# Down-projection weights in runs of four neighbouring rows per partition, with strided PE transposes to match

## The reference

```
def swiglu(h, w_gate, w_up, w_down):
    return (jax.nn.silu(h @ w_gate) * (h @ w_up)) @ w_down
...
    for e in range(N_EXPERTS):
        y = y + gates[:, e:e + 1].astype(t.dtype) * swiglu(t, w_gate[e], w_up[e], w_down[e])
```

## Time and profile before

| | us |
|---|---|
| median of 3 runs | 1413.0 (1412.39 to 1413.77) |
| the profiled execution, its time | 1415.45 |
| the profiled execution, its span | 1413.7 |
| TensorE matmul busy | 1386.3 (98%) |
| VectorE busy | 1121.7 (79%) |
| ScalarE busy | 941.2 (67%) |
| HBM read | 428.33 MB |

### The profile page before, as it was taken

How to read it: one execution, slowest core, us unless ns; L and a number is a source line. 1 busy time by engine, 2 the same in 40 slices (tenths; PEclk the granted TensorE clock), 3 DMA queues, 4 the chain that set the end, 5 groups by cost and what they waited for, 6 DMA issues and landing times. The chain is left out here.

```text
span 1413.7 us, 16873 instructions
## 1 busy us (share of the span) xinstructions
PE 1386.3 (98%) x6454; PEld 1118.3 (79%) x6454; DVE 1121.7 (79%) x1298; ACT 941.2 (67%) x1248; POOL 123.7 (9%) x117
## 2 busy tenths in 40 slices
PE   7999999999999999999999999999999999999998
PEld 4886788886786788888888888888888888887886
DVE  2565545553655599999999899999999999999996
ACT  3544534443545387887787787787887788779773
POOL 2041000001031100000000040000001000000600
PEclk9999999999999999999999999999999999999999
DMA  9324555527114599999999999999999999999992
GB/s 355 121 97 157 200 188 188 198 78 295 49 72 178 192 393 394 390 395 397 391 393 395 388 393 395 395 393 394 393 397 395 394 392 393 394 395 397 396 390 103
DMA packets 180680, 435.25 MB, mean 308 GB/s; under 512 B 5556, under 2 KB 10356, under 8 KB 180468
## 3 DMA queue, kind: packets, MB, share of 16 engines
q1 hardware_dynamic: 177540, 423.11, 79.7%
q0 software_dynamic: 3056, 11.02, 2.0%
HBM read 428.33 MB, written 5.78 MB: 307 GB/s over the span
## 5 line engine op out<-in xcount | busy, mean ns | idle before, releaser
L2100 DVE TENSOR_TENSOR unit_rounded<-wmem,unit_rounded 128x1024 fp32r<-128x1024 f32 (+1 forms) x744 | 851.9, 1206 | 56.3 <-ACT unit_rounded L1484 55.3
L1484 ACT ACTIVATE unit_rounded<-wmem 128x1024 fp32r<-128x1024 f32 (+1 forms) x744 | 719.9, 1044 | 120.0 <-PE ps L1162 46.5
L1023 PE MATMUL ps<-unit_rounded,vbuf_rounded 128*128 128x512 f32 x472 | 184.1, 390 | 0.0
L1025 PE MATMUL ps<-unit_rounded,stage_rounded 128*128 128x512 f32 x472 | 183.9, 390 | 0.0
L1024 PE MATMUL ps<-unit_rounded,vbuf_rounded 128*128 128x512 f32 x472 | 183.8, 389 | 0.0
L1160 PE MATMUL ps<-unit_rounded,hT_rounded 128*128 128x512 f32 x448 | 177.7, 397 | 0.0
L1162 PE MATMUL ps<-unit_rounded,hT_rounded 128*128 128x512 f32 x448 | 174.9, 390 | 0.0
L1161 PE MATMUL ps<-unit_rounded,hT_rounded 128*128 128x512 f32 x448 | 174.6, 390 | 0.0
L1160 PE MATMUL ps<-unit_rounded,qkT_rounded 128*128 128x512 f32 x336 | 133.4, 397 | 0.8 <-DVE qkT_rounded L2289 0.8
L1162 PE MATMUL ps<-unit_rounded,qkT_rounded 128*128 128x512 f32 x336 | 131.1, 390 | 0.0
L1161 PE MATMUL ps<-unit_rounded,qkT_rounded 128*128 128x512 f32 x336 | 131.0, 390 | 0.0
(11 more groups left out here) (286 smaller groups left out, 1781.8 us busy)
## 6 DMA issues: line engine op xcount, KB each, us to landing
wmem<-in_w_exp_gate_dram SPq DMA_DIRECT2D x56, 2048.0 KB, 12.6
wmem<-in_w_exp_up_dram SPq DMA_DIRECT2D x56, 2048.0 KB, 13.2
wmem<-in_w_exp_down_dram SPq DMA_DIRECT2D x56, 2048.0 KB, 13.2
wmem<-in_w_in_dram SPq DMA_DIRECT2D x4, 3072.0 KB, 17.3
wmem<-in_w_ff_up_dram SPq DMA_DIRECT2D x5, 2048.0 KB, 8.9
wmem<-in_w_ff_gate_dram SPq DMA_DIRECT2D x5, 2048.0 KB, 7.6
wmem<-in_w_ff_down_dram SPq DMA_DIRECT2D x5, 2048.0 KB, 7.6
wmem<-in_w_out_dram SPq DMA_DIRECT2D x4, 2048.0 KB, 8.0
```

The costliest lines, as they stand in the source:

```text
L1023: pe.matmul(o, hhb, hi[:, b, c], start=(first and b == 0), stop=False, skip_group_check=True)
L1025: mm = pe.matmul(o, hlb, hi[:, b, c], start=False, stop=(b == blocks - 1), skip_group_check=True)
L1484: act.activation(quarter_r(HIGH[l][0 if last else kind], q, cols), quarter(SETS[l][i][kind], q, cols), ACT.Copy).then_inc(hi_ready[kind], 1)
L2100: dve.tensor_tensor(quarter_r(u, q, cols), quarter(u, q, cols), quarter_r(HIGH[l][0 if last else kind], q, cols), ALU.subtract).then_inc(l ...
```

## The change

The 512 rows of a down piece are dealt to the partitions in runs: partition p gets rows `4p` to `4p + 3`, which are neighbours in memory, so its 16 KB are one contiguous piece in HBM and in SBUF. In the dense step with 256 rows it is two rows and 8 KB. Slot k of the partitions then holds rows `4p + k`. So that the hidden columns on the partitions are the same rows, block b of the transposes reads the columns `b, b + 4, b + 8, ...` of `hid` (every second column in the small dense step) in place of 128 neighbours. Gate and up loads, the matmuls, the writes to PSUM and everything else stay.

```diff
+        def dealt(a, cols, b):
+
+            return a[:, 0:cols].rearrange("t (p k) -> t k p", p=P)[:, b, :]
...
             def load_down(w, l, i, f0, rows=FT):
-                sp.dma_start(unit(SETS[l][i][2], rows // P, D), w[f0:f0 + rows, :].rearrange("(k p) c -> p k c", p=P)) \
+                sp.dma_start(unit(SETS[l][i][2], rows // P, D), w[f0:f0 + rows, :].rearrange("(p k) c -> p k c", p=P)) \
                     .then_inc(s_raw[i][2], 16)
...
                 if kind < 2:
                     dst = unit(SETS[1][i][kind], KD, FT)
-                    src = (w_exp_gate, w_exp_up)[kind][0, ds(e, 1), :, f0:f0 + FT]
+                    src = (w_exp_gate, w_exp_up)[kind][0, ds(e, 1), :, f0:f0 + FT].rearrange("o (k p) c -> p (o k) c", p=P)
                 else:
                     dst = unit(SETS[1][i][2], FT // P, D)
-                    src = w_exp_down[0, ds(e, 1), f0:f0 + FT, :]
-                sp.dma_start(dst, src.rearrange("o (k p) c -> p (o k) c", p=P)).then_inc(s_raw[i][kind], 16)
+                    src = w_exp_down[0, ds(e, 1), f0:f0 + FT, :].rearrange("o (p k) c -> p (o k) c", p=P)
+                sp.dma_start(dst, src).then_inc(s_raw[i][kind], 16)
...
                 for b in range(cols // P):
-                    mm = pe.transpose(ps[:, 2 * bufs, b * P:(b + 1) * P], hid[bufs][:, b * P:(b + 1) * P], ident)
+                    mm = pe.transpose(ps[:, 2 * bufs, b * P:(b + 1) * P], dealt(hid[bufs], cols, b), ident)
                 mm.then_inc(t_full, count)
...
                 for b in range(FT // P):
-                    mm = pe.transpose(ps[:, 2 * (m % 2), b * FEW:(b + 1) * FEW], hid[m % 2][0:FEW, b * P:(b + 1) * P],
+                    mm = pe.transpose(ps[:, 2 * (m % 2), b * FEW:(b + 1) * FEW], dealt(hid[m % 2][0:FEW, :], FT, b),
                                       ident[0:FEW, 0:FEW])
                 mm.then_inc(t_full, 2)
```

## The result

The changed kernel takes **1418.24 us** (median of 6 runs, 1417.71 to 1419.16); the kernel before, beside it, 1413.11 us (6 runs, 1412.39 to 1413.77). The ratio is 1.0031, 95% interval 1.0021 to 1.0041: slower by 0.3%, 5.1 us by the medians. The prediction said 1414.8 and that no difference would be seen. The time lies in its range of 1411 to 1441, but that range reached so far up only for a rival, a load at a quarter of the rate, that did not come; above the forecast's own 1417.5 the prediction had no case that fits.

A forecast was written before the change was run, and what follows sets the result against it. The prediction took TensorE to bound the kernel, with the DMA just behind. Its terms, -0.6 us for loads and +2.4 for transposes, gave +1.8: 1417.25 us on the profiled execution, 1414.8 against the median; range 1411 to 1441.

The forecast's parts named there:

- a load at a quarter of the rate: Rival: strided transpose loads take 228 ns and outlast their stream, +26.9 us, 1439.9 us; chance 0.22.
- the forecast's own 1417.5: Upper end of the forecast's own range from 1411.5 us, set by a strided load of 120 ns.
- What bounds the kernel: Expert stage: TensorE sets the time, DMA just behind; DMA gains mostly hidden, TensorE losses not; gathers costed at 0.
- The loads: 56 expert down loads at 427 GB/s, giving back 13.5 us of DMA time, nearly all hidden; -0.6 us paid out.
- The term for the last step: Last step: down piece lands 0.24 us earlier, shortening TensorE's wait before the last transposes; -0.6 us.
- The rival of slower long pieces: Down loads take 0.5 us longer each and the DMA sets the pace; +20, 1433 us; chance 0.05.
- the one without any effect on the DMA: Rival: down pieces are cut to 4 KB on their way, only transposes count; +2.4, 1415.4 us; chance 0.05.
- The rival of a larger gain: Whole last-step gap and half the other VectorE waits go, stride free; -3.4, 1409.6 us; chance 0.08.
- The transposes: Strided loads of `hid` at half the rate, mostly covered by the transposes' streams; +2.4 us together.
- a load that takes 111 ns beside a stream of 109 costs 2 ns: Transposes outside the few steps: 240 strided loads barely outlast their streams; 0.5 us.
- first loads without cover: First transpose load of a group that waited for VectorE: 9 at 50 ns, 0.5 us.
- few steps: Steps with short transposes of 64 identity columns: 28 strided loads at 50 ns more each, 1.4 us.

The follow-up runs named there:

- after: The changed kernel, with 16 KB down pieces and strided transposes, against the kernel before: 1418.24 us, ratio 1.0031.
- e1: The kernel before, unchanged and measured again: 1413.38 us, ratio 0.9999.
- e3: Changed kernel with its transposes reading neighbouring columns again, so only the down loads differ from the kernel before: 1413.32 us, ratio 0.9999.
- e4: Changed kernel with runs of two rows, 8 KB pieces and transposes reading every second column: 1419.36 us, ratio 1.0035 against the kernel before.
- e2: Changed kernel with the old 4 KB down loads, so only the strided transposes differ from the kernel before: 1418.81 us, ratio 1.0034.
- e5: Kernel before with strided transposes in the seven few steps alone, old loads: 1415.29 us, ratio 1.0011.
- e6: Kernel before with strided transposes in the dense and normal steps alone, old loads: 1415.91 us, ratio 1.0015.
- e9: Changed kernel with 6 identity products (12 matmuls) in the last few step's wait for VectorE: 1415.96 us, ratio 1.0016 against the kernel before.

## Why the prediction came out as it did

**What bounds the kernel**: right. TensorE had no slack and paid for everything that was not covered; VectorE and ScalarE took nearly the same time; no wait at the gathers appeared.

**The loads**: right that they would be cheaper and that this would be hidden. Forecast was 427 GB/s for a down piece, measured 422, so 10 us of DMA time and not 13.5; the queue stays flat at 11 us in after, as said, though part of that comes from the slower TensorE. The term for the last step failed: it was put at -0.6 us by a landing 0.24 us earlier, and the last piece lands no earlier (8.84 us against 8.83), while the gap is as short in e1, without the change, as in after. The rival of slower long pieces is excluded by the 422 GB/s, the one without any effect on the DMA by that and by the count of packets. The rival of a larger gain fell with e3, which has the loads without the stride and is at 0.9999, at least 0.9990.

**The transposes**: here the forecast failed, in the term "a load that takes 111 ns beside a stream of 109 costs 2 ns". The mechanism, half the rate, was right. The size was taken from ordinary loads at 77 us, (77.34 - 77.12) / 2 = 0.11; one by one they are 110 to 113 ns apart, but they are loads of other operands, and nothing shows that what sets their pace has to do with a stride. Twice the row of the loads themselves, 2 x 61 = 122 ns, was at hand, and 120 is what was measured. Nine nanoseconds decide it, because the price is the excess over 109: most of 240 loads at 10 to 12 ns and not at 2. The terms one by one: inside the groups of L1012 0.5 predicted, 1.3 measured; first loads without cover 0.5 predicted for nine, 0.2 measured, at four that cost 57 ns each; the matmul behind a group nothing predicted, 0.7 measured at 61 places; few steps 1.4 predicted, 1.6 measured, 0.4 of it behind the groups. Sum +2.4 predicted, +3.9 measured. The prediction had named the point itself ("where a load takes longer than about 116 ns"), with a rival behind it that asked for a quarter of the rate. That rival's place was right and its size was not: the case in between, a load of 120 ns, stood only as the edge of the forecast's own range, 1417.5 us, when it was the likeliest by the 61 ns row. The prediction's own signs said so too: the transposes were to stay 109 to 113 ns apart and are at 119 to 122.

**The rule on lines**: the prediction weighed "SBUF — State Buffer", its note on cachelines in the Trainium skill, by which two hits on a line of 16 bytes hide the access. e4 has two hits per line and the same loads, 207 ns in the median against 210 in e2 and 139 contiguous. The measurement decides: for these loads a second hit on the line hides nothing.

**The clock**: no step of the prediction had it; by its own last sentence it is wrong if the 0.23 us of an ordinary matmul move, and for 3.4 us they did. The rows read held a warning, the wait of TensorE of 1.4 us, behind which 64-column transposes ran; but the clock of before was at 1.00 there, and nothing in its trace showed that it was near a fall. It cost +1.6 us, nearly a third of the loss, and carried the time out of the forecast's own range, which ended at 1417.5. But the stride alone, +3.9 us, is already over the 2.8 us that count as a difference, so the likeliest case was missed by the first error, not by this one.

**What stays open**: why the clock falls in after, e2 and e4 and not in e5 or e6, where the same wait is there but comes 1.4 to 2.4 us earlier by the count from the clock's first record. Shown is only that the drop is gone when the wait is filled. Not tried: the kernel before with the wait moved later, which would tell time from stride; strides of three words, and transposes laid between large matmuls, whose own stream of 0.23 us would cover a load of 120 ns.

## What to carry to other kernels

Here a strided stationary operand was loaded at half pace, at strides of two and of four words alike. Set 2 x the pace of the contiguous load, from the distances in the trace, against the stream that covers it, and where TensorE is the bound expect to pay the difference times the count, and once more for the matmul behind each group. Put a permutation where it is free: here in the reads of PSUM by ScalarE and VectorE. And DMA time given back is worth only the waits for it that the profile shows on the bounding engine, however many microseconds of transfer it is. And before a gap that became shorter is booked as a gain, look at the same gap in a second profile of the old kernel.

## What the runs showed of the hardware that was not expected

- The stationary load of 128 columns of float32 takes 61 ns contiguous, 120 ns at a stride of 8 bytes and 120 ns at 16.
- The records of loads give the length of one (138 and 200 to 215 ns), of which the pace can't be read; distances must be used.
- TensorE's clock fell to 1.2 GHz behind a wait of only 1.4 us and four transposes of 64 columns, for 3.4 us, in after, e2 and e4, and stayed at 2.4 GHz in e9, where 12 small matmuls filled that wait at the same time. The same wait at an earlier time did not bring it in before, e1, e5 or e6.
- Reads of PSUM at a stride of 16 bytes cost VectorE (680 against 679 ns) and ScalarE (598 against 599 ns) nothing.
- Loads in pieces of 16 KB move at 422 GB/s here, in pieces of 4 KB at 407; each 16 KB piece is one packet.
- One gap at the end, behind the last load, differs by up to 1.0 us between kernels and by 0.4 us between two profiles of the same kernel (2.05 and 1.64).
